# Gate matrices of a PEER layer by one 256-column matmul a token, their one-hots divided anew among three engines, groups spread over blocks 41 to 123

## What is computed

```python
def chunk(c):
    xc = lax.dynamic_slice_in_dim(xt, t0, C, axis=0)
    ec = lax.dynamic_slice_in_dim(experts, t0, C, axis=0)   # 128 expert numbers a token
    gc = lax.dynamic_slice_in_dim(gate, t0, C, axis=0)      # their softmax weights
    u = expert_u[ec]
    a = jax.nn.gelu(jnp.einsum('cd,ced->ce', xc, u).astype(jnp.float32), approximate=False)
    return jnp.einsum('ce,ced->cd', (gc * a).astype(x.dtype), expert_v[ec])
```

## Time and profile before

| | us |
|---|---|
| median of 3 runs (lowest, highest) | 1032.17 (1032.04, 1032.56) |
| the profiled execution | 1032.03 |
| its span in the trace | 1030.0 |
| busy in the span: PE, PEld | 1016.0, 894.2 |
| busy: DVE, ACT, POOL | 742.2, 432.2, 107.1 |

### The profile page before, as it was taken

The page is one execution under the profiler, slowest core; times in us unless marked ns, Lnnn a source line. Parts: engine busy times, 40 slices in busy tenths (PEclk is TensorE's granted clock), DMA queues, the critical chain, the costliest instruction groups (busy, mean ns, idle before and its releaser), DMA issues.

```text
span 1030.0 us, 17462 instructions
## 1 busy us (share of the span) xinstructions
PE 1016.0 (99%) x6514; PEld 894.2 (87%) x6514; DVE 742.2 (72%) x1798; ACT 432.2 (42%) x763; POOL 107.1 (10%) x210
## 2 busy tenths in 40 slices
PE   9999999999999999999999999999999999999996
PEld 3478865999999999999999999988888888888885
DVE  1165543788999679999999975566666666666667
ACT  1245432233444755555555544443333334343441
POOL 1000000004000143333333300000000000000000
PEclk9999999999999999999999999999999999999999
DMA  9742200793555544444444455576555555555551
GB/s 334 308 162 105 83 21 0 223 343 122 183 182 182 179 155 136 141 144 144 143 136 138 139 164 184 185 245 214 195 193 196 190 197 188 200 188 200 187 181 42
DMA packets 48755, 176.52 MB, mean 171 GB/s; under 512 B 5136, under 2 KB 6176, under 8 KB 47520
## 3 DMA queue, kind: packets, MB, share of 16 engines
q1 hardware_dynamic: 48272, 173.82, 49.5%
q0 software_dynamic: 400, 1.58, 0.4%
HBM read 174.33 MB, written 1.05 MB: 170 GB/s over the span
## 4 chain that ended last, share of the span: by engine, by line
PE 97%; DVE 1%; DMA 1%; ACT 0%; SPq 0%; issue 0%; DVEq 0%
PE ps L464 95%; PE ps L643 1%; DMA arena<-in_w_tok 1%; DVE xs L1676 0%; DVE xs L1670 0%; DVE arena L1664 0%; DVE xs L1661 0%; PE ps L683 0%; PE ps L543 0%; PE ps L712 0%; PE ps L532 0%; ACT slab L973 0%; ACT arena L969 0%; SPq L358 0%; PE ps L847 0%
## 5 line engine op out<-in xcount | busy, mean ns | idle before, releaser
L464 PE MATMUL ps<-x1hl,hi 128*128 128x256 f32 x2216 | 377.7, 285 | 0.0
L464 PEld LDWEIGHTS ps<-x1hl,hi 128*128 128x128 f32 x2216 | 327.3, 192 | 0.0
L464 PE MATMUL ps<-hi,ahl 128*128 128x512 f32 x992 | 265.3, 389 | 0.0
L1114 ACT CAST hi<-slab 128x1024 fp32r<-128x1024 f32 x128 | 135.2, 1056 | 204.6 <-PE ps L464 204.4
L464 PEld LDWEIGHTS ps<-hi,ahl 128*128 128x128 f32 x992 | 186.2, 188 | 38.6
L464 PE MATMUL ps<-x1hl,lo 128*128 128x256 f32 x688 | 194.6, 283 | 0.0
L1626 DVE TENSOR_TENSOR lo<-slab,hi 128x1024 fp32r<-128x1024 f32 x128 | 156.0, 1219 | 0.0
L464 PE MATMUL ps<-lo,ahl 128*128 128x512 f32 x496 | 152.7, 389 | 0.0
L464 PEld LDWEIGHTS ps<-x1hl,lo 128*128 128x128 f32 x688 | 131.7, 191 | 0.0
L1405 DVE TENSOR_TENSOR lo<-slab,hi 128x1024 fp32r<-128x1024 f32 x86 | 106.1, 1233 | 16.3 <-ACT hi L1001 16.2
L464 PE MATMUL ps<-arena 128*128 128x128 f32 (+6 forms) x806 | 111.6, 293 | 1.9 <-DVE arena L1156 1.4
(11 more groups left out here) (201 smaller groups left out, 822.9 us busy)
## 6 DMA issues: line engine op xcount, KB each, us to landing
slab<-in_pv SPq DMA_DIRECT2D x128, 512.0 KB, 3.3
slab<-in_uT SPq DMA_DIRECT2D x107, 512.0 KB, 3.3
arena<-in_wq SPq DMA_DIRECT2D x32, 512.0 KB, 5.7
ahl_raw<-in_uT SPq DMA_DIRECT2D x21, 512.0 KB, 3.3
arena<-in_w_tok SPq DMA_DIRECT2D x2, 2048.0 KB, 16.7
arena<-in_w_out SPq DMA_DIRECT2D x1, 4096.0 KB, 13.3
arena<-in_w_tok SPq DMA_DIRECT2D x4, 512.0 KB, 8.3
arena<-in_w_tok SPq DMA_DIRECT2D x1, 1792.0 KB, 19.0
```

What stands on the lines that cost most here:

```text
L464: return nc.tensor.matmul(o, lhsT, rhs, start=start, stop=stop, skip_group_check=True)
L1114: nc.scalar.copy(hi[:, v_hi_slot(c), :], raw[:, v_slot(c), :]).then_inc(v_hi, 1)
```

## The change

A token's weighted one-hot is now split too: `tbl` holds four numbers a token (row number, column number, and the weight's rest and its rounded part), and a `pair` is 256 columns, the row one-hot times the rest beside the row one-hot times the rounded part. One fp32r matmul of 256 columns a token makes two products, which have to be added. In a group of four tokens VectorE makes two pairs (one scalar_tensor_tensor of 256 elements each). For the other two GpSimd makes a plain one-hot, and ScalarE scales it twice. GpSimd makes the four plain column one-hots (`hot2`) as well. A group takes two banks, in three places (GB = 3). ScalarE copies the low products out of PSUM (`save_low`), and VectorE adds the high ones and multiplies by what lies in G for the blocks that are done already (three instructions in place of one; nothing has to be filled with ones now). Gelu is written in two parts: tokens whose gates are there to `gel`, the rest straight to G. Groups no longer come in each block from 41 to 104: group g is at block 41 + g * 21 // 16, the last at 123, so 83 blocks hold 64 groups. One buffer of the ring of weights is given up (UR = 5), and loads of the second loop have other waits at its start.

```diff
-POOL_HOT = 2
 GN = S // 4
-UR, UH = 6, 3
+UR, UH = 5, 3
 VR, VH = 8, 4
-GB = 4
+GB = 3
+DVE_PAIR, ACT_PAIR = (0, 1), (2, 3)
+GROUP_AT = [N0 + g * 21 // 16 for g in range(GN)]
...
+        hot2 = nc.alloc_sbuf_tensor_at("hot2", [P, 2, 4, P], F32R, offset=ahl_at)
+        pair = nc.alloc_sbuf_tensor_at("pair", [P, 2, 4, 2, P], F32R, offset=slab_at + 4 * 4096)
...
+        tbl = slab[:, 8320 - 4 * S:8320].rearrange("p (t a) -> p t a", a=4)
...
+        def gated_by(c):
+            return 4 * sum(at_ <= c for at_ in GROUP_AT)
...
                 if c == 0:
                     sp.wait_ge(pe_g, GN)
+                elif c == 2:
+                    sp.wait_ge(pre_gated, GN)
                 elif 4 <= c < VR:
-                    sp.wait_ge(pe_h, (NK - 1, NK, NK - 5, NK - 4)[c - 4])
+                    sp.wait_ge(pe_h, (NK - 2, NK - 1, NK, NK - 4)[c - 4])
...
             def onehots(g):
-                nc.gpsimd.tensor_copy(n2[:, g % 2, :], slotT[:, 1, 4 * g:4 * g + 4]).then_inc(n2_ready, 1)
                 if g >= 2:
                     pool.wait_ge(pe_g, g - 1)
-                pool.wait_ge(n2_ready, g + 1)
-                for q in range(POOL_HOT):
-                    ins = nc.gpsimd.tensor_scalar(hot(g)[:, 0, q, :], iota, n2[:, g % 2, q:q + 1], None, ALU.is_equal)
-                ins.then_inc(oh2_ready, 1)
...
+                for q in ACT_PAIR:
+                    ins = nc.gpsimd.tensor_scalar(pair[:, g % 2, q, 1, :], iota, tbl[:, 4 * g + q, 0:1], None, ALU.is_equal)
+                ins.then_inc(pool_first, 1)
+                for q in range(4):
+                    ins = nc.gpsimd.tensor_scalar(hot2[:, g % 2, q, :], iota, tbl[:, 4 * g + q, 1:2], None, ALU.is_equal)
+                ins.then_inc(pool_hot, 1)
...
             def gates(g):
-                pe.wait_ge(oh_ready, g + 1)
-                pe.wait_ge(oh2_ready, g + 1)
-                pe.wait_ge(oh3_ready, g + 1)
+                pe.wait_ge(dve_hot, g + 1)
+                pe.wait_ge(act_hot, g + 1)
+                pe.wait_ge(pool_hot, g + 1)
                 if g >= GB:
                     pe.wait_ge(pre_gated, g - GB + 1)
+                banks = ps[:, gate_banks(g), :]
                 for q in range(4):
-                    last = mm(ps[:, gate_bank(g), q * P:(q + 1) * P], hot(g)[:, 0, q, :], hot(g)[:, 1, q, :],
-                              q == 0, True)
+                    last = mm(banks[:, q // 2, (q % 2) * S:(q % 2 + 1) * S], hot2[:, g % 2, q, :],
+                              pair[:, g % 2, q, :, :].rearrange("p a n -> p (a n)"), q % 2 == 0, True)
                 last.then_inc(pe_g, 1)
...
-                if 0 <= c - N0 < GN:
-                    gates(c - N0)
+                for g in range(GN):
+                    if GROUP_AT[g] == c:
+                        gates(g)
...
+            def pairs(g):
+                act.wait_ge(pool_first, g + 1)
+                for q in ACT_PAIR:
+                    nc.scalar.activation(pair[:, g % 2, q, 0, :], pair[:, g % 2, q, 1, :].bitcast(F32), ACT.Copy,
+                                         scale=tbl[:, 4 * g + q, 2:3]).then_inc(act_lows, 1)
+                for n, q in enumerate(ACT_PAIR):
+                    act.wait_ge(act_lows, len(ACT_PAIR) * g + n + 1)
+                    ins = nc.scalar.activation(pair[:, g % 2, q, 1, :], pair[:, g % 2, q, 1, :].bitcast(F32), ACT.Copy,
+                                               scale=tbl[:, 4 * g + q, 3:4])
+                ins.then_inc(act_hot, 1)
+
+            def save_low(g):
+                act.wait_ge(pe_g, g + 1)
                 if g >= 2:
...
+                    act.wait_ge(pre_gated, g - 1)
+                nc.scalar.copy(low[:, g % 2], ps[:, gate_banks(g), :].rearrange("p b (q a c) -> p a c (b q)", q=2, a=2)[:, 0]
+                               ).then_inc(low_saved, 1)
...
+            def tables():
+                dve.wait_ge(rT_saved, T)
+                did(v.tensor_copy(tbl[:, :, 3].bitcast(F32R), tbl[:, :, 2]))
+                settle()
+                v.tensor_tensor(tbl[:, :, 2], tbl[:, :, 2], tbl[:, :, 3], ALU.subtract).then_inc(table_ready, 1)
+                dve.wait_ge(table_ready, 1)
+
             def onehots(g):
...
+                for q in DVE_PAIR:
+                    ins = v.scalar_tensor_tensor(out=pair[:, g % 2, q, :, :], in0=iota.unsqueeze(1).to_broadcast([P, 2, P]),
+                                                 scalar=tbl[:, 4 * g + q, 0:1],
+                                                 in1=tbl[:, 4 * g + q, 2:4].unsqueeze(2).to_broadcast([P, 2, P]),
+                                                 op0=ALU.is_equal, op1=ALU.mult)
+                ins.then_inc(dve_hot, 1)
+
+            def gate_group(g):
+                k = GROUP_AT[g]
+                high = ps[:, gate_banks(g), :].rearrange("p b (q a c) -> p a c (b q)", q=2, a=2)[:, 1]
                 a = G[:, :, 4 * g:4 * g + 4]
...
+                both_low = low[:, g % 2]
+                dve.wait_ge(low_saved, g + 1)
+                did(v.tensor_tensor(both_low[:, 0:k, :], high[:, 0:k, :], both_low[:, 0:k, :], ALU.add))
+                v.tensor_tensor(a[:, k:NK, :], high[:, k:NK, :], both_low[:, k:NK, :], ALU.add)
+                settle()
+                dve.wait_ge(gelu_done, k)
+                v.tensor_tensor(a[:, 0:k, :], both_low[:, 0:k, :], a[:, 0:k, :], ALU.mult).then_inc(pre_gated, 1)
...
+            for c in range(N0, NK + 1):
                 if filled[0] < NK:
                     fill()
...
+                for g in range(1, GN):
+                    if GROUP_AT[g] == c + 1:
+                        onehots(g)
+                for g in range(GN):
+                    if GROUP_AT[g] == c:
+                        gate_group(g)
+                if c > N0:
+                    block_gate(c - 1)
```

More of the change, by code:

```diff
@@ L394, in _ @@
             sp.wait_ge(x1_ready, 2)
-            for c in (0, 1, 4, 5):
+            for c in (0, 1, 4):
                 load_u(c)
@@ L1123, in _ @@
                     save_routes()
-                    act.wait_ge(rT_saved, T)
-                    onehot(0)
-                    fill_ones(0)
                 if c == NTURN:
-                    fill_ones(1)
-                if 0 <= c - (N0 - 1) < GN - 1:
-                    onehot(c - (N0 - 1) + 1)
+                    pairs(0)
+                for g in range(GN):
+                    if GROUP_AT[g] == c + 1:
+                        save_low(g)
+                for g in range(1, GN):
+                    if GROUP_AT[g] == c + 2:
+                        pairs(g)
+                if c + UH < NK:
+                    u_split(c + UH)
                 if c >= NK - VH:
@@ L1580, in onehots @@
                     dve.wait_ge(pe_g, g - 1)
-                for q in range(4):
-                    tok = slice(4 * g + q, 4 * g + q + 1)
-                    if q > POOL_HOT:
-                        v.tensor_scalar(hot(g)[:, 0, q, :], iota, slotT[:, 1, tok], None, ALU.is_equal)
-                    ins = v.tensor_scalar(hot(g)[:, 1, q, :], iota, slotT[:, 0, tok], slotT[:, 2, tok],
-                                          ALU.is_equal, ALU.mult)
-                ins.then_inc(oh_ready, 1)
-            def gate_group(g, blocks):
-                dve.wait_ge(pe_g, g + 1)
-                if g == 0:
-                    dve.wait_ge(ones_low, 1)
-                    dve.wait_ge(ones_high, 1)
-                    dve.wait_ge(ones_mid, 2)
-                    dve.wait_ge(gelu_done, N0)
-                if blocks:
-                    dve.wait_ge(gated, blocks)
-                a = G[:, :, 4 * g:4 * g + 4]
-                v.tensor_tensor(a, ps[:, gate_bank(g), :].rearrange("p (q c) -> p c q", q=4), a, ALU.mult
-                                ).then_inc(pre_gated, 1)
@@ L1602, in block_gate @@
-            def block_gate(c, groups):
-                dve.wait_ge(gelu_done, c + 1)
-                if groups:
-                    dve.wait_ge(pre_gated, groups)
-                else:
-                    dve.wait_ge(ones_low, 1)
-                a = arena[:, c * S:(c + 1) * S]
-                v.tensor_tensor(a, gel[:, c % 2, :], a, ALU.mult).then_inc(gated, 1)
+                for q in DVE_PAIR:
[3 more added lines that the diff above has]
+                                                 op0=ALU.is_equal, op1=ALU.mult)
@@ L1611, in _, with block_gate @@
+            def block_gate(c):
+                n = gated_by(c)
+                dve.wait_ge(gelu_done, c + 1)
+                dve.wait_ge(pre_gated, n // 4)
+                a = arena[:, c * S:c * S + n]
+                v.tensor_tensor(a, gel[:, c % 2, 0:n], a, ALU.mult).then_inc(gated, 1)
             assert filled[0] == NROUTE
@@ L1613, in _ @@
                 fill()
-            dve.wait_ge(rT_saved, T)
+            tables()
             onehots(0)
             fill()
-            for g in range(GN):
-                fill()
-                if g + 1 < GN:
-                    onehots(g + 1)
```

(22 more changed lines are left out.)

72 lines of the change are left out of this document (21 added, 51 removed).

## The result

The changed kernel takes 1052.2 us (median of 4 runs, 1051.99 to 1053.18), the kernel before, run beside it on the same chip, 1032.11 (1031.81 to 1032.56). The ratio is 1.0196 with a 95% interval from 1.0179 to 1.0214: slower by 20.1 us, 9.1 more than the forecast of 11. The profiled execution has a span of 1050.2 against 1030.0.

What follows compares the result with a forecast made beforehand. GpSimd was taken as the bound of the changed kernel: 62T + 3.84 against 296.0 us gave 9.2 or 22.1 us more; 11 was taken, near the first, so 1032.0 + 11 = 1043 us, range 1008 to 1060.

Steps and rivals of the forecast that it cites:

- Direction and mechanism: In the blocks with groups, GpSimd's one-hots wait for VectorE's SBUF reads and set the pace: slower, 0.60.
- not held: Rival: GpSimd's one-hots are not held by VectorE, TensorE stays the bound, 1006 to 1012 us; chance 0.16.
- only fills hold it: Rival: only VectorE's fills hold GpSimd's one-hots, T = 4.55 us a group, around 1022 us; chance 0.14.
- Full exclusion in both directions: Rival: GpSimd's one-hots and VectorE's two-input SBUF work add up, T = 6.47 us a group, 1141 us; chance 0.04.
- TensorE's saving: In each group, four fp32r matmuls take 0.48 us in place of 0.89; 64 groups save 26.2 us.
- The other engines: Per group, ScalarE needs 3.5 us and VectorE 3.6 to 4.2, both inside the budget of 4.26.
- T: GpSimd's time for one group's six one-hots, waits included, in us; break-even with the kernel before at 4.71.
- Groups 0 and 1 are ready by block 41. Group 2 begins 0.48 us into it.: Start of the groups: GpSimd has two groups done ahead, so 62 groups at its pace follow from there.
- the two counts: GpSimd's waits per group: first, one-hots arriving at any moment, 4.86 us a group; second, GpSimd never away, 5.07.
- The end: After GpSimd's last group, TensorE needs 0.48 + 2.88 us to the end of block 123.
- Costs nothing: VectorE's table before block 41 (some 0.8 us), ScalarE's late splits, and UR = 5 loads add no time.
- the trace's marks: Signs: matmul pitch 0.12, mean one-hot 0.75 to 0.85 us, long ones inside fills, L443 idle 35 to 45 us.

Runs made afterwards that it cites:

- Experiments 2 and 3: Changed kernel, the fill from block 42 reading its second input from PSUM: 1007.41 us; and changed kernel, column one-hots made for groups 0 and 1 only: 1007.36 us.
- experiment 1: Kernel with the layer left out: GpSimd makes one-hots or memsets while VectorE repeats one form; a one-hot takes 0.58 us with VectorE at rest, 2.36 beside fills.
- Experiment 3: Changed kernel with GpSimd making the four column one-hots for groups 0 and 1 only, later groups reusing them: 1007.36 us.
- experiment 10: Changed kernel with only ScalarE's weight splits of blocks 39 and 40 moved ahead of its scalings, six one-hots still on GpSimd: 1052.29 us, ratio 1.0194.
- the start: Edit putting ScalarE's weight splits of blocks 39 and 40 ahead of its scalings; on the changed kernel with one one-hot moved to VectorE: 1011.5 us.
- experiment 7: Changed kernel with one of the four column one-hots of a group moved from GpSimd to VectorE: 1012.36 us.
- experiment 9: Changed kernel with one column one-hot moved to VectorE and ScalarE's splits of blocks 39 and 40 ahead of its scalings: 1011.5 us, ratio 0.9799.
- experiment 5: Changed kernel with each fill from block 42 on made as two successive instructions of 512 elements: 1048.4 us.
- experiment 6: Changed kernel with VectorE's order half a fill, pair, half a fill, pair where a group comes next, whole fills elsewhere: 1039.78 us.

## Why the prediction was right and wrong

**Direction and mechanism: right.** GpSimd sets the pace; TensorE idles ahead of the group's first matmul for L443, 34.9 us (35 to 45 forecast); GpSimd is never idle. Experiments 2 and 3 show it by taking the cause away. The rival "not held" and the rival "only fills hold it" have fallen: the pair costs a one-hot 0.24 us in experiment 1 (0.82 - 0.58) and in the changed kernel (0.84 - 0.60). "Full exclusion in both directions" has fallen with the 0.09 us that VectorE loses for a one-hot.

**TensorE's saving: right.** 0.48 a group to the hundredth, 25.1 us in all by experiments 2 and 3 against 26.2.

**The other engines: right.** Forecast were 3.5 us a group on ScalarE and, at this place, some 4.0 on VectorE. Experiment 3, where TensorE sets the pace of 4.26, has them busy 84.24 and 90.97 of 100 us: 3.59 and 3.88.

**The size was off by 9 us**, and it can be laid out in full. From the place where block 41 began before (365.20) to the end of block 123 (681.04) the changed kernel needs 315.8 us against 296.0: +19.8, the whole loss. The forecast was 0.48 + 62T + 3.36 with T = 4.89. Its terms:

- *"Groups 0 and 1 are ready by block 41. Group 2 begins 0.48 us into it."* This step failed. GpSimd went from group 1 straight to group 2 at 368.60, without idle time; it had been held by three fills in a row (362.35) and was still busy with group 1 when `gates(0)` was done. 368.60 - 365.20 = 3.40 in place of 0.48: +2.9 us.
- *T.* From 368.60 to 677.35 (674.57 + 2.78) are 308.75 us for 62 groups, 4.98 each, between the two counts of 4.86 and 5.07: +5.6 us over the 4.89 that I took. The waits in it were right: 4.98 less six bare one-hots is 1.50 us, and the forecast had 4.89 - 3.39 = 1.50. Their parts fit too: from the 384 sorted above, the fills make 84 x 0.83 / 64 = 1.09 us a group (1.10 by the first count) and the shorter forms 0.41 (0.36). That the sum agrees to the hundredth is luck, since 4.89 was picked between waits of 1.47 and 1.68. The bare one-hot was mis-sized: 0.58 and not 0.565. Two in the earlier trace rows were read from the start of the first to the start of the copy behind them, 1.13, and the copy begins 0.05 us before the one-hot's end, where a one-hot behind a one-hot begins 0.02 before it. The difference counts six times a group: 6 x 0.015 x 62 = 5.6.
- *The end.* The last group starts 0.26 us behind GpSimd's last one-hot, and takes 0.55 after its wait: 677.35 to 681.04 are 3.69 in place of 3.36: +0.3.

11 + 2.9 + 5.6 + 0.3 = 19.8.

**"Costs nothing": wrong in its reason, right in its sum.** The fill of block 40 did come late, by ScalarE's split waiting behind the scalings, which waited for GpSimd (0.70 us at 360.09 after 2.71 idle): TensorE lost 1.1 us of idle time there, and block 41 began at 366.84 in place of 365.20. The prediction had covered VectorE's table with TensorE's 8 us of work, and of the split it said that it can be late only when TensorE waits for GpSimd already. Here it was late by GpSimd's first pair, while TensorE waited for the fill. It costs nothing (experiment 10), because GpSimd's chain doesn't pass through block 41. Once GpSimd is relieved it seems to cost: with one one-hot moved, the start brings 1012.36 - 1011.5 = 0.9 us. That is hardly more than repeats differ by, but the trace agrees: the one wait for L1405, 0.9 us, is there in experiment 7 and gone in experiment 9.

**By the trace's marks.** The mean one-hot of 0.84 was inside the 0.75 to 0.85 named, and the long ones begin inside fills. A held one-hot does delay the first pair behind it, by 0.11 us (below); the forecast had 0.06 for any delay of VectorE.

## What to carry to other kernels

Before work is moved to GpSimd, count what VectorE reads from SBUF in the same time, and look for like instructions in a row, not at GpSimd's idle share: here 64% of idle time (36% busy) could not hold four more one-hots a group, though their bare time fitted. An engine that is to be filled over 80% needs its bare pitch to a hundredth of a microsecond, since it is multiplied by every instruction of the stretch, and the first groups have to be written out one by one. Where the share-out is that near, moving one small instruction is worth more than the whole change: 0.31 us on VectorE turned +20 us into -20.

## What was unexpected in the hardware

- A held GpSimd instruction isn't always let in at the end of the VectorE instruction that holds it. In a row of 1024-element fills a one-hot takes 2.36 us, two fills, and in experiment 5 78 of 80 one-hots waited past the end of the first half to that of the second. Where another form follows, as in experiment 6 and beside the alternating forms of experiment 1, it gets in at the first end. The longest one-hot in the changed kernel, 2382 ns, stands at the start, where three fills follow each other without a gap. The row of pairs, 0.82 us for two of 0.41, doesn't need a missed end to be explained: the 0.5 us that a one-hot needs once it is let in are longer than a pair. Why an end is missed, the runs don't show.
- An instruction of VectorE with a single input of 1024 elements (0.66 us) holds GpSimd too: 1.98 us a one-hot.
- GpSimd's memset, which reads nothing, isn't held: 1.92 us for four with VectorE at rest and 1.93 beside the fills.
- A wait of TensorE costs more than its row says: 0.17 us of draining and 0.07 at the restart, and a delay of 0.13 us has no row at all.
- VectorE's two pairs at 523.25 take 0.91 us, not 2 x 0.41: the first, which begins while a held one-hot has just been let in, takes 0.51 and the second 0.40. In experiment 3, 43 first pairs beside such a one-hot have a mean pitch of 0.51, and the 20 with GpSimd idle 0.40.
